# Two gate products in one stage, earlier loads for two stages, and the head maxima ahead of the convolution

## The reference

```python
q, k, v, rw, gl = jnp.split(h @ w_in, IN_SPLITS, axis=-1)
ya = latent_window_attention(q, k, v, kc, vc, sink)
r_l, v_l, hg_l, kk_l, dirs_l = rwkv_prepare(short_conv(rw, conv_w), ...)
# in rwkv_prepare:
kk = heads(k * k_k)
kk = kk * lax.rsqrt(jnp.maximum(jnp.sum(kk * kk, axis=-1, keepdims=True), 1e-24))
w_log = -jax.nn.softplus(-(decay_w0[d] + jnp.tanh(hw) @ decay_w2[d])) - 0.5
a = jax.nn.sigmoid(iclr_a0[d] + ha @ iclr_a2[d])
# the recurrence wkv7_scan over tokens in two directions, then
ga, gr = jnp.split(jax.nn.sigmoid(gate_logits), N_BRANCHES, axis=-1)
return (ga * (ya @ w_branch_attn) + gr * (yr @ w_branch_rwkv)) @ w_out
```

## Time and profile before

| | us |
|---|---|
| median of 3 runs | 4740.95 (4729.24 to 4745.95) |
| the profiled execution, its own time | 4736.67 |
| its span, first to last instruction | 4734.9 |
| PE busy | 4130.6 (87%) |
| DVE busy | 2731.4 (58%) |
| ACT busy | 1748.5 (37%) |
| POOL busy | 329.5 (7%) |
| mean granted TensorE clock | 0.923 |

### The profile page before, as it was taken

The page is one execution under the profiler, slowest core; times in us unless marked ns, Lnnn a source line. Parts: engine busy times, 40 slices in busy tenths (PEclk is TensorE's granted clock), DMA queues, the critical chain, the costliest instruction groups (busy, mean ns, idle before and its releaser), DMA issues. The chain is left out here.

```text
span 4734.9 us, 81944 instructions
## 1 busy us (share of the span) xinstructions
PE 4130.6 (87%) x34438; PEld 3392.6 (72%) x34438; DVE 2731.4 (58%) x4351; ACT 1748.5 (37%) x2865; POOL 329.5 (7%) x415
## 2 busy tenths in 40 slices
PE   6999986997898998699478897978999587999997
PEld 5878864886785667488366676768888466888886
DVE  2347736884774554789345013657777644466556
ACT  2136623774463442377346111223222112222222
POOL 0000000220000000021000000023233001000000
PEclk9999996998999999799689898969898789999998
DMA  2100037994000002899300201000000031111110
GB/s 100 45 9 2 2 114 292 376 397 147 19 2 1 1 13 98 314 397 382 124 20 19 89 30 59 25 8 3 3 3 3 26 142 54 45 54 36 54 45 40
DMA packets 139161, 425.62 MB, mean 90 GB/s; under 512 B 14660, under 2 KB 50380, under 8 KB 114220
## 3 DMA queue, kind: packets, MB, share of 16 engines
q1 hardware_dynamic: 129580, 386.83, 21.2%
q0 software_dynamic: 9216, 33.56, 2.8%
HBM read 370.03 MB, written 50.33 MB: 89 GB/s over the span
## 5 line engine op out<-in xcount | busy, mean ns | idle before, releaser
L557 PE MATMUL psum<-weight_parts,h_parts 128*128 128x512 f32 (+2 forms) x2880 | 601.0, 371 | 46.0 <-DVE weight_parts L703 29.6
L557 PEld LDWEIGHTS psum<-weight_parts,h_parts 128*128 128x128 f32 x2880 | 508.2, 192 | 132.9 <-DVE weight_parts L703 30.7
L1520 DVE TENSOR_TENSOR weight_parts<-weights_raw,weight_parts 128x2048 fp32r<-128x2048 f32 x192 | 431.8, 2288 | 57.5 <-ACT weight_parts L1490 55.4
L911 ACT ACTIVATE scores<-scores,softmax_stats 128x1024 f32<-128x1024 f32 (+2 forms) x288 | 307.9, 1069 | 329.7 <-DVE softmax_stats L956 329.6
L1490 ACT ACTIVATE weight_parts<-weights_raw 128x2048 fp32r<-128x2048 f32 x192 | 360.6, 1919 | 76.8 <-DMA weights_raw<-in_moe_w_up 46.1
L1428 PE MATMUL psum<-weight_parts,picked_parts 128*128 128x512 f32 x1536 | 365.0, 398 | 16.1 <-DVE weight_parts L1520 10.8
L1901 PE MATMUL psum<-h_parts,up_parts 128*128 128x512 f32 x1536 | 355.5, 393 | 11.0 <-DVE up_parts L1976 11.0
L1917 PE MATMUL psum<-down_parts,hidden_parts 128*128 128x512 f32 x1536 | 353.5, 391 | 6.7 <-DVE down_parts L1981 6.7
L1428 PEld LDWEIGHTS psum<-weight_parts,picked_parts 128*128 128x128 f32 x1536 | 291.5, 191 | 80.1 <-issue 11.5
L703 DVE TENSOR_TENSOR weight_parts<-weights_raw,weight_parts 128x2048 fp32r<-128x2048 f32 (+2 forms) x48 | 100.7, 2098 | 426.5 <-ACT weight_parts L612 426.5
L1901 PEld LDWEIGHTS psum<-h_parts,up_parts 128*128 128x128 f32 x1536 | 291.7, 190 | 72.5 <-DVE up_parts L1976 11.8
(11 more groups left out here) (437 smaller groups left out, 7243.1 us busy)
## 6 DMA issues: line engine op xcount, KB each, us to landing
weights_raw<-in_moe_w_gate SPq DMA_DIRECT2D x64, 1024.0 KB, 14.0
weights_raw<-in_moe_w_up SPq DMA_DIRECT2D x64, 1024.0 KB, 14.1
weights_raw<-in_moe_w_down SPq DMA_DIRECT2D x64, 1024.0 KB, 13.0
w_ada<-in_w_ada SPq DMA_DIRECT2D x12, 2048.0 KB, 11.2
up_raw<-in_w_mlp_up SPq DMA_DIRECT2D x16, 1024.0 KB, 7.2
down_raw<-in_w_mlp_down SPq DMA_DIRECT2D x16, 1024.0 KB, 4.9
weights_raw<-in_even_w_in SPq DMA_DIRECT2D x10, 1024.0 KB, 5.1
weights_raw<-in_w_in SPq DMA_DIRECT2D x10, 1024.0 KB, 5.2
```

What stands on the lines that cost most here:

```text
L557: last = pe.matmul(ps[:, t, 0:width(n)], cols[:, i, KP * h + k, t * P:(t + 1) * P], part[:, n % 2, j, k, 0:width(n)], start=(h == 0 and m ...
L911: act.activation(s_b[:, i % 2, a, 0:w], s_b[:, i % 2, a, 0:w], ACT.Exp, bias=st[:, i % 4, 0, a:a + 1], scale=-1.0, accum_out=st[:, i % 4, ...
L1520: dve.tensor_tensor(part[:, n % PART_SLOTS, 1], raw[:, n % RAW_SLOTS], part[:, n % PART_SLOTS, 0].bitcast(F32), ALU.subtract).then_inc(low, 1)
```

## The change

- The two gate products become one `project` call with four spans, the recurrent gate first. Spans 2 and 3 overwrite the buffer halves of spans 0 and 1, so ACT waits before each of them for the store of that half (`stored_twice`).
- The weights of steps 0 and 1 of `rwkv` are loaded in the branch stage, by its `loads`, into a buffer of their own, `first_weights_raw`. DVE waits for these loads before its first evacuation there. SP starts the `rwkv` stage with steps 2 and 3.
- On DVE, the three maxima of a key tile come ahead of the step's convolution. The reciprocal of steps 4 to 7 stays in front of both.
- The four lora loads go first among the twelve, on a semaphore of their own. PE waits for these four, DVE for the eight others.

```diff
 def project(...)
+    kept_spans = len(spans) // 2 if stored_twice else len(spans)
...
-            if store:
+            if store and not stored_twice:
                 for s in range(max(0, len(spans) - 2), len(spans)):
                     store_span(s)
-                sp.wait_ge(stored, 16 * len(spans))
+            if store:
+                sp.wait_ge(stored, 16 * kept_spans)
...
                     if loads and s == 0:
                         act.wait_ge(loads_done, 16 * len(loads))
+                    if stored_twice and s >= kept_spans:
+                        act.wait_ge(stored, 16 * (s - kept_spans + 1))
...
 def second_block(c, x, xf)
-    project(c, hP, w_in, gate_spans(3488), 86, 102, lambda a: True, sigmoid_of(3488),
-            store=(rows_of("g_scratch"), gate))
-    project(c, hP, w_in, gate_spans(2464), 86, 102, lambda a: True, sigmoid_of(2464))
+    project(c, hP, w_in, gate_spans(3488) + gate_spans(2464), 86, 102, lambda a: True, sigmoid,
+            store=(rows_of("g_scratch"), gate), stored_twice=True)
+    first_raw = c.at("first_weights_raw", 166, [P, 2, KT, P])
+    w_cols = w_in.rearrange("(k p) n -> p k n", p=P)
     project(c, y_parts, dram["w_branch_attn_2"][0], spans, 86, 102, lambda a: False,
...
-            store=(rows_of("h_scratch"), gate))
+            store=(rows_of("h_scratch"), gate),
+            loads=[(first_raw[:, i], w_cols[:, :, 768 + (4 + i) * P:768 + (5 + i) * P]) for i in (0, 1)])
...
 def rwkv(...), SP
             for p, j in enumerate(order):
+                if p >= 4:
+                    sp.wait_ge(low, p - 1)
                 if p >= 2:
-                    sp.wait_ge(low, p - 1)
-                sp.dma_start(raw[:, p % 2, :, 0:widths[j]], w_rows[:, :, starts[j]:starts[j] + widths[j]])\
-                  .then_inc(loaded[p % 2], 16)
-                if p == 1:
+                    sp.dma_start(raw_of(p)[:, :, 0:widths[j]], w_rows[:, :, starts[j]:starts[j] + widths[j]])\
+                      .then_inc(loaded[p % 2], 16)
+                if p == 3:
                     sp.dma_start(blocks[:], dram["const_head_blocks"]).then_inc(blocks_loaded, 16)
...
 ACT
-                act.wait_ge(loaded[p % 2], 16 * (p // 2 + 1))
                 if p >= 2:
+                    act.wait_ge(loaded[p % 2], 16 * (p // 2))
                     act.wait_ge(summed, before[p - 1])
...
 DVE: the block "if 0 <= p - 1 - K_AT < 4" with the maxima moves
+                (ahead of) dve.wait_ge(copied, before[p + 1]) and the three taps
-                (from behind) dve.nop().then_inc(convolved, 1)
...
 def scan(...)
-            for to, source in loads:
+            for to, source in loads[:4]:
+                sp.dma_start(to, source).then_inc(lora_loaded, 16)
+            for to, source in loads[4:]:
                 sp.dma_start(to, source).then_inc(tables_loaded, 16)
-            pe.wait_ge(tables_loaded, 16 * len(loads))
+            pe.wait_ge(lora_loaded, 64)
-            dve.wait_ge(tables_loaded, 16 * len(loads))
+            dve.wait_ge(tables_loaded, 16 * (len(loads) - 4))
```

More of the change, by code:

```diff
@@ L1812, in second_block, with sigmoid @@
     gate = c.at("gate_rows", 134, [P, TILES, D])
-    def sigmoid_of(start):
-        return lambda a, b, t, act, p, step: act.activation(gate[:, t, a - start:b - start], p, ACT.Sigmoid)
-    project(c, hP, w_in, gate_spans(3488), 86, 102, lambda a: True, sigmoid_of(3488),
-            store=(rows_of("g_scratch"), gate))
-    project(c, hP, w_in, gate_spans(2464), 86, 102, lambda a: True, sigmoid_of(2464))
+    def sigmoid(a, b, t, act, p, step):
+        col = (a - 2464) % D
+        return act.activation(gate[:, t, col:col + b - a], p, ACT.Sigmoid)
+    project(c, hP, w_in, gate_spans(3488) + gate_spans(2464), 86, 102, lambda a: True, sigmoid,
+            store=(rows_of("g_scratch"), gate), stored_twice=True)
+    first_raw = c.at("first_weights_raw", 166, [P, 2, KT, P])
+    w_cols = w_in.rearrange("(k p) n -> p k n", p=P)
     project(c, y_parts, dram["w_branch_attn_2"][0], spans, 86, 102, lambda a: False,
             lambda a, b, t, dve, p, step: dve.tensor_tensor(gate[:, t, a:b], p, gate[:, t, a:b], ALU.mult), kt=4,
-            store=(rows_of("h_scratch"), gate))
-    yr = rwkv(c, hP, hc, w_in, conv, vT)
+            store=(rows_of("h_scratch"), gate),
+            loads=[(first_raw[:, i], w_cols[:, :, 768 + (4 + i) * P:768 + (5 + i) * P]) for i in (0, 1)])
+    yr = rwkv(c, hP, hc, w_in, conv, vT, first_raw)
     m = c.at("merged_rows", 118, [P, TILES, D])
@@ L2024, in _, with rwkv @@
             dve.wait_ge(added, 16 * steps)
-def rwkv(c, h, hc, w_in, conv, vT):
+def rwkv(c, h, hc, w_in, conv, vT, first_raw):
     nc, dram, ps = c.nc, c.dram, c.psum
@@ L2046, in rwkv @@
     raw = c.at("weights_raw", 86, [P, 2, KT, P])
+    raw_of = lambda p: first_raw[:, p] if p < 2 else raw[:, p % 2]
     part = c.at("weight_parts", 94, [P, 2, 2, KT, P], F32R)
@@ L2130, in split @@
                 n = widths[order[p]]
-                act.wait_ge(loaded[p % 2], 16 * (p // 2 + 1))
                 if p >= 2:
+                    act.wait_ge(loaded[p % 2], 16 * (p // 2))
                     act.wait_ge(summed, before[p - 1])
-                act.activation(part[:, p % 2, 0, :, 0:n], raw[:, p % 2, :, 0:n], ACT.Copy).then_inc(high, 1)
+                act.activation(part[:, p % 2, 0, :, 0:n], raw_of(p)[:, :, 0:n], ACT.Copy).then_inc(high, 1)
             split(0)
@@ L2197, in _ @@
                                                   ALU.mult, ALU.mult))
+                if 0 <= p - 1 - K_AT < 4:
+                    i = p - 1 - K_AT
+                    for q, (a, b) in enumerate(pieces):
+                        dve.wait_ge(key_summed, 3 * i + q + 1)
+                        dve.tensor_scalar(rw[:, i, a:b], ps[:, 6 + (3 * i + q) % 2, 0:b - a], 1e-24, None, ALU.max)\
+                           .then_inc(key_maxed, 1)
                 dve.wait_ge(copied, before[p + 1])
@@ L2206, in _ @@
                 dve.nop().then_inc(convolved, 1)
-                if 0 <= p - 1 - K_AT < 4:
-                    i = p - 1 - K_AT
-                    for q, (a, b) in enumerate(pieces):
-                        dve.wait_ge(key_summed, 3 * i + q + 1)
-                        dve.tensor_scalar(rw[:, i, a:b], ps[:, 6 + (3 * i + q) % 2, 0:b - a], 1e-24, None, ALU.max)\
-                           .then_inc(key_maxed, 1)
     y = c.at("y_rows", 58, [P, TILES, 512])
@@ L2225, in rwkv @@
         masks.append(k)
-    loads = [(keep[:], dram["const_chunk_starts"][:, 0:256]), (eye[:], dram["const_chunk_identity"])]
+    loads = [(w2[32 * i:32 * i + 32, d], dram[name][0, d]) for d in (0, 1)
+             for i, name in ((0, "decay_w2_2"), (1, "iclr_a2_2"))]
+    loads += [(keep[:], dram["const_chunk_starts"][:, 0:256]), (eye[:], dram["const_chunk_identity"])]
     for d, k in enumerate(masks):
@@ L2356, in scan @@
     both = [f"{n}_{i}" for i in range(4) for n in names]
-    with stage(nc, "dve_step", "tables_loaded", *both) as (block, dve_step, tables_loaded, *sems):
+    with stage(nc, "dve_step", "lora_loaded", "tables_loaded", *both) as (
+            block, dve_step, lora_loaded, tables_loaded, *sems):
         sem = [dict(zip(names, sems[i * len(names):(i + 1) * len(names)])) for i in range(4)]
```

9 lines of the change are left out of this document (4 added, 5 removed).

## The result

The changed kernel takes 4686.8 us (median of 4 runs, 4670.1 to 4692.9), the kernel before, measured beside it, 4735.1 (median of 4, 4727.1 to 4746.0). The medians are 48.3 us apart. The ratio is 0.9893, with an interval of 0.9878 to 0.9908: 50.7 us of 4735, between 43.6 and 57.8. The execution with a profile took 4681.4 us, its span is 4679.6 us, against 4734.9 before.

A forecast was written before the change was run, and what follows sets the result against it. PE was taken to set the pace, losing time standing still and at a lower clock. Savings of 20.8 + 3.7 + 25.9 + 2.8 = 53.2 us from the median 4740.95 gave 4687.8, range 4672 to 4702.

The forecast's parts named there:

- Gates, forecast 20.8: Border between the two gate products: 17.65 us of PE wait and 3.2 us of lower clock go, between 17.6 and 20.9.
- the new wait on ACT: Before spans 2 and 3 ACT waits for a store issued 43.5 us earlier; claimed to cost nothing.
- The slow clock behind the border: Second gate product: 90.2 us against 87.04 for 32 tiles and pieces, so 3.2 us of lower clock would go.
- First weights, forecast 3.7: Start of the recurrent input stage: ACT splits without waiting for SP's load, 3.7 us of 14.49 go; bounds 0 to 3.7.
- Maxima, forecast 25.9: Four key rounds of the recurrent input stage: 92.1 us become 66.2, 25.9 us saved; bounds 18.8 to 26.8.
- the round without wait: Key round on PE: 1.88 + 0.66 + 13.78 us of units, in all 16.3; 16.4 with 0.1 us of wait left.
- Lora, forecast 2.8: Start of the recurrence: PE starts 3.7 us earlier, but DVE waits for the last table, so 2.8 us; bounds 0 to 3.7.
- That only the waits go (2): All four places: waits go but the clock terms don't come back; 42.9 us saved, time 4698, chance 0.10.
- DVE as the bound (3): Key rounds: DVE becomes the bound and late weights cost up to 3.7 us a round; sum 38.4, time 4703, chance 0.06.
- The stage waiting for its stores (4): Merged gate stage waits for its stores at the old border, some 6 us; 47 us saved, time 4694, chance 0.03.
- Another clock in the recurrence (5): Recurrence: its moved start changes its clock, 9.5 us for one stretch more or less; 4678 or 4697, chance 0.07.
- a sign that it was wrong: Recurrence: more than 10 us longer or shorter than its 620 us would show the prediction wrong.

The follow-up runs named there:

- the part alone: Under gates: kernel before with only the gate products in one stage, 4716.05 us, ratio 0.9964; under first weights: kernel before with only those loads moved, 4729.3 us.
- the kernel with extra matmuls: Kernel before with 20 extra matmuls between the second and third key sum of each key tile, filling PE's 4.7 us wait; 4732.9 us in one execution.
- brought about by hand: Changed kernel with PE waiting, before its first matmul of span 2, for the stores of both halves; 4694.4 us in one execution.

## Why the prediction was right

**The total.** 4687.8 was predicted and 4686.8 measured, but that the two are 1 us apart is partly luck: the kernel before came out at 4735.1 when it was run again, not at 4740.95. Taken from 4735.1, the sum of 53.2 us gives 4681.9, 5 us under the measured median. The fair comparison is between the savings: 53.2 forecast, 54.2 and 54.0 in the stretches of the two traces, 50.7 (43.6 to 57.8) by the ratio of the times.

**Gates, forecast 20.8.** 20.8 in the trace of the change, 19.8 in its second, 20.1 in the part alone. The step that could have gone wrong was the new wait on ACT. The prediction put the store two pieces, 43.5 us, ahead of it. It is three pieces and a tile, since sums are evacuated only while the second piece of a span is worked on. In the changed kernel that made 67.4 us:

```profile
2699.10 0.37 SPq L473 DMA_DIRECT2D g_scratch<-gate_rows  x1
...
2766.53 0.60 ACT L1820 ACTIVATE gate_rows<-psum 128x512 f32<-128x512 f32 x1 [22.14 <-PE psum L559]
```

The slip was on the safe side, and ACT didn't wait for the store. These are all waits of ACT from 2600 to 2800 in the changed kernel (who waited for whom, us in total, times, longest), for PE and for loads, none for `g_scratch`:

```profile
ACT gate_rows L1820 <- PE psum L559: 82.4, 31, 22.1
ACT weight_parts L614 <- PE psum L559: 62.8, 3, 24.0
ACT weight_parts L614 <- DMA weights_raw<-in_w_in: 7.9, 2, 7.4
ACT weight_parts L614 <- DMA weights_raw<-in_w_branch_attn: 6.5, 2, 5.9
```

The slow clock behind the border went too, 3.2 us as read from the earlier trace rows. The Trainium skill (TensorE: Matmul & The Clock Gate, "The HAM clock gate") says of a kernel's start that the number of slow matmuls there varies from run to run, and advises against fitting it. The traces here bear that out for the start of a stage. Five kernels still have the border. In them the second gate product, from its first matmul to its last evacuation, took 90.27, 90.18, 89.26, 90.11 and 90.09 us, against 87.04 at full clock: the restart cost 2.2 to 3.2 us, and the prediction had read the highest of the five. The first gate product's start scatters in the same way, by 1.5 us over the ten traces, and that is why the whole stretch without a border took 187.1, 187.8 and 188.1 us. So the mechanism was right, the term is good to about 1 us, and that it came out to the tenth in the first trace is luck.

**First weights, forecast 3.7.** The wait fell by 3.70 us, from 14.49 to 10.79. The stretch fell by 3.38 with the whole change and by 3.7 with the part alone.

**Maxima, forecast 25.9.** 27.5: this is the term that was mis-sized, by 1.64 us, and it lies outside the prediction's own bounds for it, 18.8 to 26.8, the upper of which stood for no wait left. The step that failed is the round without wait, "1.88 + 0.66 + the units", and with it the 1.26 us until DVE sees a sum. Both prices came from rows in which PE ran at the low clock, behind the very wait that was to vanish. At the full clock the units follow 0.35 us behind the third sum (2908.20 to 2908.55 in the kernel with extra matmuls), and DVE sees a sum after 1.05 us (2883.34 to 2884.39). So the third sum starts 1.05 + 0.69 + 0.06 = 1.80 us after the first instead of 1.97, and the key sums take 2.15 us instead of 2.63. Against that, the units took 13.97 and not 13.78. The round is 16.12 instead of 16.4. The three rounds without the reciprocal make up half of the 1.64 us. The other half is the reciprocal: it ended at 2932.70, when the first sum was just being seen (2931.68 + 1.05 = 2932.73), and cost 0.1 us and not 0.6.

**Lora, forecast 2.8.** 2.83, and the releaser named was the one that showed.

**The rivals.** That only the waits go (2) fell with the extra matmuls: 8.6 us were clock, and the change, whose rounds have the clock at 1.00, got them back. DVE as the bound (3) fell: PE waits for no weight split in the recurrent input stage behind its start, and DVE's longest turn ended 0.1 us too late. The stage waiting for its stores (4) didn't come about, but brought about by hand it cost 9.7 us where the rival had priced 6: the landing takes 7.1 and not about 6, PE was waiting from a moment before the issue, and the restart at the low clock, 1.9 us, was left out. Another clock in the recurrence (5) is real, but in every kernel: 609.9 to 630.2 us, where the prediction called over 10 us from 620 a sign that it was wrong. It isn't one, since the changed kernel alone showed 616.4 and 630.2. It widens the scatter of single executions; the medians of the kernel before lay at 4732.4 to 4737.9 in the three comparisons.

## What to carry to other kernels

A wait of TensorE cost more than its length here: behind it the engine ran at the low clock, which took about 2 us for each of four waits of 4.7 us, 1.9 for one of 7.75 and 2.2 to 3.2 for one of 17.65. Shortening a wait to 4.6 us or more gave back only what it was shortened by; taking it away gave back the clock too. Where PE sets the pace, it pays to count its waits one by one, borders of stages included, and to take away what they wait for by loading one stage earlier or by letting DVE serve the one that holds PE before its long work. And durations for the forecast of a dense stretch have to be read from rows at the clock that it will have, not from the rows next to the wait.

## What the runs showed of the hardware

- Short waits and the clock. Four waits of 4.7 us, one in each round of about 23 us, held the granted clock at 0.87 over 92 us; the same stretch without them has 1.00. They cost 8.55 us on top of their 18.8. A single wait of 7.75 us cost 1.9 us behind it. One of 17.65 us at the same place cost 2.2 to 3.2 in five traces: the price of a restart scatters by about 1 us with the same work.
- The granted clock of a long stretch of small matmuls scatters by itself. The recurrence, with small matmuls and POOL, ACT and DVE between them, took 609.9 to 630.2 us with the clock at 0.90 to 0.84, for the same instructions. Why it is granted 0.84 once and 0.88 the next time in the same kernel stays open: the code ahead is the same, and the stage starts only 0.9 us later. Whoever compares two traces of such a kernel has to compare stretch by stretch first.
